# Modulation panels summed on VectorE instead of TensorE, in the buffer of the tokens

## What is computed

```python
def modulation(cond, w_mod, b_mod):
    m = jax.nn.silu(cond) @ w_mod + b_mod          # w_mod: 2048 x 6144
    m = m.reshape(-1, 1, 3 * D_MODEL)
    return jnp.split(m, 3, axis=-1)
...
for layer in range(DEPTH):                         # DEPTH = 2
    shift, scale, gate = modulation(c, w_mod[layer], b_mod[layer])
    shift_c, scale_c, gate_c = modulation(c_ctx, w_mod[layer], b_mod[layer])
    h = rms_norm(x, norm_w[layer]) * (1.0 + scale) + shift
    hc = rms_norm(xc, norm_w[layer]) * (1.0 + scale_c) + shift_c
    # projections, attention, gate unit, out projection: y, y_c
    x = x + gate * y
    if not last:
        xc = xc + gate_c * y_c
```

## Time and profile before

| | |
|---|---|
| median of 3 runs | 3623.99 us (3620.34 to 3625.52) |
| the profiled execution | 3621.41 us, its span 3619.6 us |
| TensorE busy in the span | 94% |
| VectorE / ScalarE / GpSimd busy | 54% / 51% / 12% |
| granted TensorE clock, mean | 0.974 |

### The profile page before, as it was taken

The page is one execution under the profiler, slowest core; times in us unless marked ns, Lnnn a source line. Parts: engine busy times, 40 slices in busy tenths (PEclk is TensorE's granted clock), DMA queues, the critical chain, the costliest instruction groups (busy, mean ns, idle before and its releaser), DMA issues.

```text
span 3619.6 us, 60203 instructions
## 1 busy us (share of the span) xinstructions
PE 3411.6 (94%) x25613; PEld 3065.3 (85%) x25613; DVE 1956.6 (54%) x2697; ACT 1846.3 (51%) x2906; POOL 434.0 (12%) x592
## 2 busy tenths in 40 slices
PE   6899999999899999999999999999989999899798
PEld 2577777778688999999999989999989899788797
DVE  1423222232455455666666465555576555899756
ACT  1344433322456744767766345555455564676444
POOL 0010101101000000000000010000010002688301
PEclk9999999999999999999999999999999999899899
DMA  9654555532233455555554545455545345333354
GB/s 384 220 174 141 170 178 190 200 124 98 76 123 128 157 175 176 169 192 178 171 188 157 182 158 175 169 169 168 170 147 169 123 136 180 114 127 129 106 180 146
DMA packets 157963, 589.83 MB, mean 163 GB/s; under 512 B 18352, under 2 KB 18384, under 8 KB 156032
## 3 DMA queue, kind: packets, MB, share of 16 engines
q1 hardware_dynamic: 135216, 497.64, 40.7%
q0 software_dynamic: 21904, 86.24, 7.0%
q10 hardware_dynamic: 576, 2.10, 0.2%
HBM read 583.69 MB, written 2.21 MB: 162 GB/s over the span
## 4 chain that ended last, share of the span: by engine, by line
PE 64%; PEld 12%; DVE 10%; DMA 6%; ACT 5%; issue 3%; PEldq 0%; POOL 0%; DVEq 0%; SPq 0%; ACTq 0%; POOLq 0%
PE psum_all L513 18%; PE psum_all L515 17%; PE psum_all L517 17%; PEld psum_all L517 4%; PEld psum_all L513 4%; PEld psum_all L515 4%; DMA raw<-in_stream 4%; DVE w_lo L459 2%; DMA mod_early<-in_stream 2%; PE psum_all L725 2%; ACT w_hi L452 1%; PE psum_all L1333 1%; DVE s_vd L2912 1%; PE psum_all L1303 1%; DVE s_vb L2911 1%
## 5 line engine op out<-in xcount | busy, mean ns | idle before, releaser
L513 PE MATMUL psum_all<-act_hi,w_hi 128*128 128x256 f32 (+1 forms) x6704 | 2055.6, 307 | 73.6 <-DVE act_lo L884 46.4
L515 PE MATMUL psum_all<-act_lo,w_hi 128*128 128x256 f32 (+1 forms) x6704 | 2019.0, 301 | 0.0
L517 PE MATMUL psum_all<-act_hi,w_lo 128*128 128x256 f32 (+1 forms) x6704 | 2017.6, 301 | 0.0
L459 DVE TENSOR_TENSOR w_lo<-raw,w_hi 128x1024 fp32r<-128x1024 f32 x866 | 1077.6, 1253 | 1248.0 <-ACT w_hi L452 1246.2
L513 PEld LDWEIGHTS psum_all<-act_hi,w_hi 128*128 128x128 f32 x6704 | 1293.9, 193 | 170.7 <-issue 101.7
L452 ACT ACTIVATE w_hi<-raw 128x1024 fp32r<-128x1024 f32 x866 | 910.5, 1057 | 854.7 <-DMA raw<-in_stream 852.6
L515 PEld LDWEIGHTS psum_all<-act_lo,w_hi 128*128 128x128 f32 x6704 | 1294.9, 193 | 42.5 <-issue 3.4
L517 PEld LDWEIGHTS psum_all<-act_hi,w_lo 128*128 128x128 f32 x6704 | 1293.5, 193 | 42.0
L699 POOL DMA_DIRECT2D mod_late<-in_stream x128 | 67.6, 532 | 660.5 <-PE psum_all L725 557.5
L961 POOL TENSOR_TENSOR ln_acc<-xT 128x256 f32<-128x256 f32 x8 | 5.9, 737 | 1018.2 <-DVE xT L1698 1018.2
L644 PE MATMUL psum_all<-mod_early,s_silu 128*32 128x512 f32 x256 | 57.6, 639 | 29.4 <-DMA mod_early<-in_stream 29.1
(11 more groups left out here) (475 smaller groups left out, 3316.6 us busy)
## 6 DMA issues: line engine op xcount, KB each, us to landing
raw<-in_stream SPq DMA_DIRECT2D x866, 512.0 KB, 3.3
mod_late<-in_stream POOLq DMA_DIRECT2D x128, 512.0 KB, 5.1
mod_early<-in_stream SPq DMA_DIRECT2D x64, 512.0 KB, 8.9
ssd_seg<-acs_rows POOLq DMA_DIRECT2D x8, 1536.0 KB, 6.7
ctxT<-in_ctx SPq DMA_DIRECT2D x2, 2048.0 KB, 13.9
xT<-in_x SPq DMA_DIRECT2D x1, 2048.0 KB, 15.9
fox_key_cum<-cum_rows POOLq DMA_DIRECT2D x1, 2048.0 KB, 8.7
out<-xT SPq DMA_DIRECT2D x4, 512.0 KB, 2.6
```

The source lines that it names most:

```text
L459: dve.tensor_tensor(w_lo[:, n % RING, :], raw[:, n % RING, :], w_hi[:, n % RING, :].bitcast(F32), ALU.subtract).then_inc(lo_ready, 1)
L513: pe.matmul(sums, w_hi[:, n % RING, cols], block.rhs(kk, True, block.width), start=(kk == 0), stop=False)
L515: pe.matmul(sums, w_hi[:, n % RING, cols], block.rhs(kk, False, block.width), start=False, stop=False)
L517: last = pe.matmul(sums, w_lo[:, n % RING, cols], block.rhs(kk, True, block.width), start=False, stop=(kk == block.kt - 1))
```

## The change

The eight late panels are no longer multiplied by TensorE. VectorE forms, for each condition, the sum over the 16 units of unit times the condition's column (a scalar for each partition): `tensor_scalar` for the first, `scalar_tensor_tensor` for the others. The sums (128x1024, one or two conditions, two panels in turn) stand in `xT`, whose tokens have been used. For panels 4 and 5 of layer 1 (the gate) only the tokens' condition is summed. Four units after a panel's last pair TensorE adds up each sum's 128 rows, with the sum as stationary operand and one column of ones moving: 8 matmuls for each condition, in PSUM. ScalarE has no part in it, and the banks aren't cleared. The pairs are spread over 80 units in place of 84. When all is summed, GpSimd's queue loads the context, and after the last turn the tokens, and `add_gated` waits for both.

```diff
-LATE_SLOTS = 84
+LATE_SLOTS = 80
+LATE_LAG = 4
...
-            if name == "gate_in0":
-                out.append(("ctx", 0))
...
-                    if g < late:
-                        for n in units_of(g):
-                            late_scalar(act, n)
...
-        late_rows = [norm_root, at_work("mod_late_rows", [P, 256], 80)]
+        late_sums = [[xT[:, 8 * s + 4 * v:8 * s + 4 * v + 4, :].rearrange("p k t -> p (k t)") for v in range(2)]
+                     for s in range(2)]
+        late_summed = sem("late_summed")
...
-        def clear_late(dve):
-            for bank in (6, 7):
-                dve.memset(psum[bank], 0.0)
+        def late_conditions(p):
+            return 1 if LATE_PAIRS[p * PAIRS][0:2] in ((1, 4), (1, 5)) else 2
+        def late_sums_before(m):
+            return sum(late_conditions(i // KT) for i in range(m))
+        def wait_late_used(eng, m):
+            eng.wait_ge(late_summed, late_sums_before(m + 1))
 
         def late_loads(pool):
             pool.wait_ge(stage_done, 4 * late_stages)
             for m in range(2 * len(LATE_PAIRS)):
                 if m >= LATE_RING:
-                    pool.wait_ge(mod_multiplied, len(EARLY_PAIRS) * 2 + m - LATE_RING + 1)
+                    wait_late_used(pool, m - LATE_RING)
                 u = mod_units(*LATE_PAIRS[m // 2])[m % 2]
                 pool.dma_start(late_units[:, m % LATE_RING, :], ins["stream"][u]).then_inc(late_landed[m % LATE_RING], 16)
 
+            wait_late_used(pool, 2 * len(LATE_PAIRS) - 1)
+            pool.dma_start(ctxT[:, :, :], ins["ctx"]).then_inc(ctx_landed, 16)
+            pool.wait_ge(mod_turned, 12)
+            pool.dma_start(xT[:, :, :], ins["x"]).then_inc(ctx_landed, 16)
+
+        def late_turned(slot):
+            return panel_ended(slot - LATE_LAG)
 
         def late_tensor(pe, slot):
-            p = panel_ended(slot - 1)
+            p = late_turned(slot)
             if p is not None:
-                pe.wait_ge(mod_rows_ready, 4 + 2 * p + 2)
-                for b in range(4):
-                    last = pe.matmul(psum[6 + p % 2][:, 4 * b:4 * b + 4],
-                                     late_rows[b // 2][:, (b % 2) * P:(b % 2) * P + P], small[:, 0:4],
-                                     start=True, stop=True)
+                pe.wait_ge(late_summed, late_sums_before((p + 1) * KT))
+                if p >= 2:
+                    pe.wait_ge(mod_added, 4 + p - 1)
+                for v in range(late_conditions(p)):
+                    for h in range(2):
+                        for b in range(4):
+                            at = 4 * b + 2 * h + v
+                            last = pe.matmul(psum[6 + p % 2][:, at:at + 1],
+                                             late_sums[p % 2][v][:, (4 * h + b) * P:(4 * h + b + 1) * P],
+                                             const("ones", 0, 1), start=True, stop=True)
                 last.then_inc(mod_turned, 1)
+        def late_add(dve, i):
+            p = i // PAIRS
+            n = late_conditions(p)
+            for m in (2 * i, 2 * i + 1):
+                k, done = m % KT, late_sums_before(m)
+                dve.wait_ge(late_landed[m % LATE_RING], 16 * (m // LATE_RING + 1))
+                if k == 0 and p >= 2:
+                    dve.wait_ge(mod_turned, 4 + p - 1)
+                for v in range(n):
+                    sums, unit = late_sums[p % 2][v], late_units[:, m % LATE_RING, :]
+                    if k == 0:
+                        dve.tensor_scalar(sums, unit, s_late[:, k, v:v + 1], None, ALU.mult).then_inc(late_summed, 1)
+                    else:
+                        dve.wait_ge(late_summed, done - n + v + 1)
+                        dve.scalar_tensor_tensor(out=sums, in0=unit, scalar=s_late[:, k, v:v + 1], in1=sums,
+                                                 op0=ALU.mult, op1=ALU.add).then_inc(late_summed, 1)
+
+        def late_vector(dve, slot):
             i = pair_after(slot)
             if i is not None:
-                late_multiply(pe, i)
...
+                late_add(dve, i)
+            p = late_turned(slot)
             if p is not None:
                 layer, in_layer = LATE_PAIRS[p * PAIRS][0:2]
-                mod_add(dve, layer, in_layer, 4 + p, 6 + p % 2)
+                mod_add(dve, layer, in_layer, 4 + p, 6 + p % 2, late_conditions(p))
...
             mod_scale(dve, 0, 4)
-            clear_late(dve)
...
-                        dve.wait_ge(ctx_landed, 16)
+                        dve.wait_ge(ctx_landed, 32)
...
-                if kind == "ctx":
-                    sp.wait_ge(mod_multiplied, 12 * KT)
-                    sp.wait_ge(mod_turned, 12)
-                    sp.dma_start(ctxT[:, :, :], ins["ctx"]).then_inc(ctx_landed, 16)
-                    continue
```

More of the change, by code:

```diff
@@ L662, in mod_turn, with mod_add @@
             last.then_inc(mod_turned, 1)
-        def mod_add(dve, layer, p, panel, bank=5):
+        def mod_add(dve, layer, p, panel, bank=5, conditions=2):
             dve.wait_ge(mod_turned, panel + 1)
             a = layer * 96 + p * 16
-            out = modulation[:, a:a + 16].rearrange("p (h b v) -> p b h v", h=2, v=2)
-            bias = param("b_mod", a, a + 16).rearrange("p (h b v) -> p b h v", h=2, v=2)
-            dve.tensor_tensor(out, psum[bank][:, 0:16].rearrange("p (b h v) -> p b h v", h=2, v=2), bias, ALU.add) \
-               .then_inc(mod_added, 1)
+            out = modulation[:, a:a + 16].rearrange("p (h b v) -> p b h v", h=2, v=2)[:, :, :, 0:conditions]
+            bias = param("b_mod", a, a + 16).rearrange("p (h b v) -> p b h v", h=2, v=2)[:, :, :, 0:conditions]
+            sums = psum[bank][:, 0:16].rearrange("p (b h v) -> p b h v", h=2, v=2)[:, :, :, 0:conditions]
+            dve.tensor_tensor(out, sums, bias, ALU.add).then_inc(mod_added, 1)
         def mod_scale(dve, layer, panels_added):
@@ L711, in late_tensor @@
+        def late_vector(dve, slot):
             i = pair_after(slot)
             if i is not None:
-                late_multiply(pe, i)
-        def late_multiply(pe, i):
-            p, pair = i // PAIRS, i % PAIRS
-            bank = psum[6 + p % 2]
-            if pair == 0 and p >= 2:
-                pe.wait_ge(mod_added, 4 + p - 1)
-            for e in range(2):
-                m = 2 * i + e
-                pe.wait_ge(late_landed[m % LATE_RING], 16 * (m // LATE_RING + 1))
-                for h in range(2):
-                    rows = slice(32 * (2 * e + h), 32 * (2 * e + h) + 2)
-                    last = pe.matmul(bank[rows, :], s_late[:, 2 * pair + e, :],
-                                     late_units[:, m % LATE_RING, h * 512:(h + 1) * 512],
-                                     start=(pair == 0), stop=(pair == PAIRS - 1))
-                last.then_inc(mod_multiplied, 1)
@@ L730, in late_scalar @@
-        def late_scalar(act, slot):
-            p = panel_ended(slot)
-            if p is not None:
-                act.wait_ge(mod_multiplied, (4 + p + 1) * KT)
-                if p:
-                    act.wait_ge(mod_turned, 4 + p)
-                for h in range(2):
-                    act.activation(late_rows[h][:, :], psum[6 + p % 2][:, h * 256:(h + 1) * 256], ACT.Copy) \
-                       .then_inc(mod_rows_ready, 1)
-        def late_vector(dve, slot):
-            p = panel_ended(slot - 1)
+                late_add(dve, i)
```

## The result

| | before | after |
|---|---|---|
| median of 4 runs each, side by side | 3624.68 us (3620.34 to 3625.52) | 3563.12 us (3559.81 to 3565.32) |
| the profiled execution | 3621.41 us, its span 3619.6 us | 3563.67 us, its span 3561.7 us |

The ratio is 0.9833, with an interval of 0.9819 to 0.9848: the changed kernel is 1.7% faster, 61.6 us by these medians. The forecast was 3573 us, its range 3556 to 3598. A second comparison on another chip (experiment 9) gave 3565.6 against 3623.32 us.

The account below looks back on a forecast made before the run. TensorE was taken to pace layer 0's projections. Its -59 us (-70 - 13 + 24), -1 for clears and +9 of waits give -51: 3570 from 3621.4, 3573 as median, range 3556 to 3598.

Parts of the forecast that it names:

- What leaves TensorE: Layer 0's projections: panel matmul pairs save 70 us, old turns and their waits for row copies 13 us.
- What TensorE gets: Panel turns in layer 0: 112 one-column matmuls at 0.2 us, with entering and leaving 24 us.
- The prediction's last sentence: Prediction is wrong if TensorE waits over 2 us a head, passes exceed 1.5 us, or waits lower the 0.99 clock.
- VectorE's passes: Panel sums in layer 0: 224 passes at a pitch of 1.19 us, 267 us; VectorE at 83% of the stage.
- VectorE's waits: TensorE waiting on VectorE's queue order in heads and early blocks: +9 us, with 0 and +30 as ends.
- The 3 us allowed for the early blocks: Early attention blocks: 3 us of wait, since each k head has a 3.35 us reciprocal on top.
- The 0.7 us a head: Attention heads: TensorE waits 0.7 us a head on average for VectorE's normalised probabilities.
- The edits at no cost: Two PSUM clears dropped at stage start give -1 us; late units, context and token loads, ScalarE's fewer copies stay hidden.
- That it paces everything: Rival: VectorE paces the whole stage and is slower, 3673 us at 2.1 us a pass; chance 0.05.
- That the transfers limit: Rival: transfers limit the stage and hide TensorE's saving, DMA share 0.57, no change at 3624 us; chance 0.03.
- The GpSimd rule: GpSimd contends with VectorE's two-input instructions; if issuing loads counted, a layer 0 pass would be 16% dearer.
- the first rival: VectorE paces the heads and early blocks, waits 30 us in place of 9, time 3594 us; chance 0.2.

Follow-up runs that it names:

- experiment 9: The changed kernel again with no edit, on another chip: 3565.6 us, ratio 0.983 to the kernel before.
- the fourth kernel: The changed kernel with each panel's turn cut to one matmul in place of 16 or 8: 3539.55 us, ratio 0.9765 to the kernel before.
- 5: The kernel before with two panel matmuls of 8 columns for a pair of units in place of four of 512: 3570.39 us, ratio 0.9847.
- a1: The changed kernel with each accumulating VectorE pass covering 16 of the 1024 columns: 3559.92 us, ratio 0.9821 to the kernel before.
- 7: The changed kernel with the tokens loaded a second time and the gating waiting for that too: 3556.62 us in a single execution.
- 2: The changed kernel with one extra accumulating VectorE pass for each unit's first condition, half as many again: 3635.26 us, ratio 1.0026 to the kernel before.
- 3: The changed kernel with an extra accumulating VectorE pass on every second unit, a quarter more: 3612.82 us in a single execution.
- 6: The changed kernel with a 128x256 GpSimd addition after each of the 128 late unit loads: 3585.08 us in a single execution.

## Why the prediction was right

**What leaves TensorE: 83 us forecast, 84 to 88 measured.** The stage became 54.4 us shorter. By the fourth kernel the turns weigh 27.2 us for 104 matmuls, 29 for 112, and by the first the waits for VectorE weigh 0.6: 54.4 + 29 + 0.6 = 84. By the pieces, 24.3 us of turns, 8.1 more for the clock, and waits of 4.6 against the old 3.6 besides the row copies': 54.4 + 24.3 + 8.1 + 1.0 = 88. The narrowed kernel before, 49.0 less for an expected 48, supports the larger part of it by itself.

**What TensorE gets: 24 us forecast, some 29 to 32 measured.** This is the term of the sum that was too small. The price of a matmul was right, 3.47 us for 16 in the chain, 0.217 each; 112 of them are 24.3. What the step lacked is mainly the time behind the turn. It took four such matmuls from the old trace, behind which nothing slows, and multiplied; sixteen in one stretch bring a lower clock for at least 3.4 us, in which matmuls take twice as long (1.73 to 3.51 us). In the stage the clock takes 8.1 us more than before, 11.6 in the second execution. The prediction's last sentence had the clock as a risk, but by way of waits.

**VectorE's passes.** 224 x 1.19 = 267 us was forecast; 256.4 + 10.0 busy were measured, in one stretch with a pitch of 1.20 us. The 14 passes that begin a panel were priced too high (749 ns), the others a little too low. The share is 77%, forecast near 80%.

**VectorE's waits: +9 us forecast, 0.6 measured.** This term was mis-sized by more, and the other way. TensorE waits 2.5 us for VectorE in the whole stage (one k, one set of probabilities), and of this 0.6 shows in the end. The 3 us allowed for the early blocks were about right: with short passes the first probabilities are turned 3.7 us sooner, and that only comes to nothing because TensorE later waits 3.1 us less for ScalarE. The 0.7 us a head were not there. The heads were put at 31.5 us and took 31.75, which looks like 0.7 us of waiting each; with the passes made short they still take 31.65, and with the turns in four parts 30.96. That the number fits is chance: the prediction started from the 33.2 us of one head, and the seven heads of the old timeline take 34.3 on average (probabilities turned from 227.12 to 467.35 us), so that its own sum for TensorE gives 31.5 without any wait. The count for VectorE was about right (25.3 us busy and 2.8 waiting for the exponentials in a head, 28.1 against 28.6, which is 89% of a head) and the conclusion too cautious: the probabilities were ready in time all the same. Where the margin ends, the runs with more sums show, and it ends sooner than a count of busy time says.

The errors of the two terms, 5 to 8 us too little and 8 too much, work against each other, so that the stage came out 4.4 us shorter than the forecast 50. That the time was met to 10 us is in part this luck; the mechanism, TensorE's queue shortened by the panels at little cost in waits, is what experiments 1 and 5 show. The rest of the 10 us between 3573 and 3563.12 is in the start (1.8 in place of 1), in the rest of the program (1.7) and in the scatter of the medians.

**The edits at no cost.** The stage begins 1.8 us sooner, forecast 1 for the two clears; the starts of the kernels without the clears lie between 110.8 and 113.6 us, so one pair of profiles doesn't show it. The late units land after 3.3 to 7.3 us, and VectorE waits 1.5 us in all for one. Context and tokens are hidden, and a second load of the tokens too.

**The rivals.** That VectorE paces the heads fell with a1. That it paces everything needs passes of 1.57 us in the heads; they take 1.28. That the transfers limit fell with the result, and with DMA engines at 0.59. The GpSimd rule would have made a pass 16% dearer: with a computing GpSimd it is 12% dearer, and the kernel is then 21.5 us slower, about what the first rival had for it (21), but GpSimd doesn't compute in this stage.

**What the profile was to show.** 224 recorded one-column matmuls: yes. Heads of 31 to 32 us: 31.75. Passes of 1.25 to 1.3: 1.28. The wait for high parts below 100: 79.9. The stage from 127 us to the last turn, 550 to 570: the last turn ends at 693, so 566. The clock was listed as something that could fall because of waits; it fell without them.

## What to carry to other kernels

Moving work from the engine that sets the pace to one that is mostly idle pays nearly in full as long as the second engine's queue keeps its due times. Adding a quarter as much work again, as an experiment, tells better than sums of busy time how near the end of that is: here the heads took 35.2 us where the sums said 33. Price what the pacing engine is given in return as the stretch in which it will stand: a row of the old trace gives the time of four small matmuls, not the time of the work behind sixteen. The faster form here spreads the turn over four units or brings the rows in first; by the medians on the same chip they took a further 15 and 17 us off (3550.6 and 3548.59 against 3565.6), by the stage 6 to 8 and 13 to 16.

## What was not expected of the hardware

- A stretch of 16 one-column fp32 matmuls with 128x128 weights each, 3.63 us on the timeline in which TensorE and its weight loads hardly pause, is followed by the clock's lower level: 24 times out of 24 in the four executions whose queues are otherwise the changed kernel's (its two profiles and those of 1 and 7), for 3.4 us in 16 of them and for 6.8 in 8. In the slower kernels 2, 3 and 6 it is 15 of 18; each of the other three stretches begins within 20 us of another fall's start. Behind a stretch of 8 (1.84 us) or of 4 (0.95 us) the clock stays at 1.00. One of the six places, at the step from the last head to the first group, has a fall in all seven kernels without such a stretch too, so only the 20 falls elsewhere speak for the stretches (12 of 15 in 2, 3 and 6). Why the chip does it isn't shown. In the turn at 569 us of the first profile the fall came before the turn's own end and made it 4.38 us long.
- `tensor_scalar` over 128x1024 fp32 takes 749 ns, `scalar_tensor_tensor` with two SBUF sources 1280 ns; eight of the latter in a row take 9.65 us, so each starts some 0.08 us before the one ahead of it has ended.
- A GpSimd addition of 128x256 (0.65 us) beside VectorE costs VectorE's two-source passes 12% on average; 128 load issues of 0.53 us cost it nothing that shows (splits of 1222 ns beside them, 1226 behind the last).
